# A hybrid decoder step on one core: squares of x spread out, latents copied early, the pool chain begun sooner

## The chip, the cores and the metric

One Trainium2 chip, one core of it. The metric is the device time of one execution in microseconds (us); the time before is the median of three runs. The engines are called TensorE (PE in the rows), VectorE (DVE), ScalarE (ACT), GpSimd (POOL) and SyncE (SP, which here only issues DMAs). PEld is TensorE's weight load.

## The reference

One layer of a decoder for 512 prompt tokens and 8 x 8 sample tokens (576 tokens in all), d_model 2048, everything in float32. What matters here is the front of it:

```
h = rms_norm(x) ; z = h @ w_in
q_a (512) | ckv (256) | krope (64) | u (512) | qm (512) | gate (2048) = split(z)
ckv = rms_norm(ckv) ; krope = rope(krope)          # the latents, outputs too
pool: per group g of 4, window w = 2, 4, 8, 16:
    diff = trailing_mean(u_g, w) - u_g ; y_g = (diff @ w_pool_g) * pool_scale
memory: k, v = split(rms_norm(mem) @ w_mem_kv)
out = x + concat(mla, pool, cross) * silu(gate) @ w_out ; final rms_norm
```

The row factor 1/rms of x is a number per token, so the kernel multiplies x (times the norm's weights) by w_in first and scales the products later. For that it needs the sum of squares of every row of x, at some time before the first scaling.

## The kernel before, in words

Every float32 product is made of three matmuls on two halves: a value is split into a high half (ScalarE copies it to the narrower matmul type) and a low half (VectorE subtracts the high half from it), and `product` (L91) adds high x high, high x low and low x high (L94 to L96). So each block of weights passes DMA, ScalarE, VectorE and TensorE in that order, through a few slots that come free when TensorE has used them.

The front stage (`front_stage`, L256) is one program per engine, written out by hand; each engine runs its own instructions strictly in order and waits on semaphores. TensorE's order is:

1. **Latents** (L957): ckv and krope for 576 tokens, six weight units, token blocks in five PSUM banks (`kv_bank`, L341). Banks 3, 4 and 5 hold three of these five.
2. Units 6 and 7, the two halves of the gate of pool group 0 (`half`, L1018).
3. **28 products** (`pair_product`, L976): 4 pairs of output blocks (q_a and u) times 7 terms, a multiplication of 2 x 2 blocks with 7 products instead of 8. The weight sums of a pair are made by VectorE (`first` to `fourth`, L714 to L744). The token side has four *turned* blocks t1 to t4: x times the norm's weights is written as four quarters q0 to q3 (`x_scaled`, 16 blocks of 128 x 576, L622 to L627, all on ScalarE), VectorE adds the quarters (`turned_sum`, L754: t1 = q1 - q0, t2 = q3 - t1, t3 = q3 - q1, t4 = q2 - t2), ScalarE makes the high halves (`turned_hi`, L570), VectorE the low ones (`turned_lo`, L768). The high halves lie on the quarters' memory, so one waits until the quarter is read. Product 2 of each pair uses t2, product 3 t1, product 4 t3 and product 6 t4. Products add into banks A, B and C, which alternate between banks 0 to 2 and 3 to 5, so pair 1 (products 7 to 13) needs the latents' banks; product 7 waits for their copies (`kv_raw`, L989). Within a pair a bank is copied out between two products: product 2 adds to bank B and waits until ScalarE's step 0 has copied what product 0 left there.
   After product 13 five small matmuls spread 1/rms over the partitions (*the broadcast*, L1048 to L1055); they wait for `x_diag` (L870), and that for the sums of squares.
4. Units idx 2 to 25 of `ORDER` (L57): halves f2 to f9 (gates of pool groups 1 to 3, cross queries) and memory units m0 to m15, with the transposes of the tails of u (L1061) and the four pool products (L1069 to L1080) between them.

ScalarE and VectorE walk through the 28 products as *steps*: at each step one bank copy or addition, then the halves of the weights of product step + 3 (`pair_hi` L575, `pair_lo` L746), then other work that is tied to a step number. ScalarE's extra work is `square_row` (L560): it waits until a 128 x 2048 row block of x has landed, squares it with a running sum, and issues the DMA of the next block, on its own queue, into the same buffer. VectorE copies the latents' banks out at step 6 (L855 to L861).

After the steps both walk through j = 5 to 27, which stands for the unit idx j. The dictionaries `DIFF_AT`, `PO_AT`, `BEND_AT` (L239 to L241) and `POOLED_AFTER` (L242) tie the pool chain to j or idx. For each group g: GpSimd adds window levels (L526 to L534), VectorE makes the difference and its halves (L914 to L930, six instructions), TensorE multiplies (after unit idx), VectorE scales the result (L908 to L913), GpSimd multiplies with gate and sigmoid (`close_gate`, L508). GpSimd begins group g + 1 when VectorE has ended the difference of group g.

Of the kernel before, what the change touches and what calls it, by code (L numbers as in the profile page):

```python
# [17 lines left out]
ALU = mybir.AluOpType  # L18
# [11 lines left out]
KD = D // P  # L30
# [206 lines left out]
SQUARE_AT = {1: 0, 4: 1, 5: 2, 6: 3, 8: 4}  # L237
Z_OUT_AT = {6: 1, 14: 2, 23: 3}
DIFF_AT = {6: 0, 13: 1, 17: 2, 20: 3}  # L239
PO_AT = {13: 0, 17: 1, 20: 2, 24: 3}  # L240
BEND_AT = {7: 0, 9: 1, 17: 2, 25: 3}  # L241
POOLED_AFTER = {9: 0, 13: 1, 16: 2, 20: 3}  # L242
# [13 lines left out]
def front_stage(nc, a, s, block):  # L256
# [3 lines left out]
    with ExitStack() as ctx:  # L260
# [119 lines left out]
        T_AT = {2: 0, 1: 1, 3: 2, 4: 3}  # L380
# [19 lines left out]
        def t_high(t):  # L400
            return thi[:, T_AT[t], :, :]

# [90 lines left out]
        def _(pool):  # L493
# [22 lines left out]
            for g in range(GR):  # L516
                if g == GR - 1:
                    close_gate(0)
# [28 lines left out]
            for g in range(1, GR):  # L547
                close_gate(g)
# [4 lines left out]
        def _(act):  # L553
# [69 lines left out]
            for k in range(KD):  # L623
                if k == 8:
                    ring_hi(KV_UNITS + 1)
                act.activation(fs[:, 2 * (k // 8):2 * (k // 8) + 2, k % 8, :], halves(xraw[:, k, :]), ACT.Identity,
                               scale=gx[:, k:k + 1]).then_inc(scaled, 1)  # L627
# [9 lines left out]
            for step in range(PRODUCTS):  # L637
# [13 lines left out]
                if step == 10:  # L651
                    act.wait_ge(chain, 1)
                    act.activation(rx[:, 2, :], rx[:, 1, :], ACT.Sqrt).then_inc(root, 1)
# [13 lines left out]
            for j in range(AHEAD + HI, FIRST + 2 - KV_UNITS):  # L667
# [7 lines left out]
                if j == 10:  # L675
# [23 lines left out]
        def _(dve):  # L699
# [54 lines left out]
            def turned_sum(t):  # L754

                if t != 1:
                    dve.wait_ge(t_sum, {2: 1, 3: 2, 4: 2}[t])
                dve.wait_ge(scaled, 8 if t == 1 else KD)
# [9 lines left out]
            def turned_lo(t):  # L768

                dve.wait_ge(st_hi, T_HI_COUNT[t])  # L770
                if t == 2:
                    dve.wait_ge(t_sum, 4)
# [35 lines left out]
            ring_lo(KV_UNITS)  # L808
            first(0)
            turned_sum(1)  # L810
            ring_lo(KV_UNITS + 1)
            second(0)
            third(0)
            turned_sum(2)
            turned_sum(3)
            pair_lo(0)
            fourth(0)
            pair_lo(1)
            turned_sum(4)
            turned_lo(2)  # L820
            pair_lo(2)
            turned_lo(1)

            for step in range(PRODUCTS):
# [30 lines left out]
                if step == 6:  # L855
                    dve.wait_ge(prep, 2)
                    dve.wait_ge(s.w_used, KV_UNITS)
                    dve.wait_ge(kv_low, 1)
                    dve.tensor_tensor(s.kvn[0:NS, 4, :], kv_bank(4)[0:NS], kv_tmp, ALU.add).then_inc(kv_raw, 1)
                    for r in range(4):  # L860
                        dve.tensor_copy(s.kvn[:, r, :], kv_bank(r)).then_inc(kv_raw, 1)  # L861
                if step == 9:
                    dve.wait_ge(sq, TT)
                    link(dve.tensor_scalar(rx[:, 1, :], rx[:, 0, :], 1.0 / D, EPS, ALU.mult, ALU.add))
                if step == 10:
# [30 lines left out]
            for j in range(AHEAD + HI, FIRST + 2 - KV_UNITS):  # L896
                if j == 8:
# [33 lines left out]
                if j == 7:  # L931
# [17 lines left out]
        def _(pe):  # L949
# [105 lines left out]
            for idx, (kind, k) in list(enumerate(ORDER))[AHEAD:]:  # L1055
# [5 lines left out]
                if idx == 6:  # L1061
# [2576 lines left out]
```

## Time and profile before

| | |
|---|---|
| median of three runs | 878.52 us (878.41 to 879.72) |
| the profiled execution's own time | 879.79 us |
| its span in the trace | 878.1 us |
| TensorE busy | 849.1 us, 97% |
| VectorE, ScalarE, GpSimd busy | 659.9, 502.3, 145.9 us |
| granted TensorE clock, mean | 0.988 of full speed |

The span is what the trace shows between the first and the last instruction; the execution's own time is 1.69 us more. Times in the rows are counted from the span's start. A matmul's row starts when it enters the engine, and rows of one engine overlap a little. In the timeline a bracket at the end of a row gives the idle time of the engine before that row and what ended it.

### The profile page before, as it was taken

How to read it: one execution, taken by the hardware profiler on the slowest of the kernel's cores; microseconds unless marked ns; L12 is line 12 of the kernel's file. 1: busy time of each engine (PE TensorE's matmuls, PEld its weight loads, DVE VectorE, ACT ScalarE, POOL GpSimd, SP SyncE). 2: the span in 40 equal slices, each digit the busy share in tenths (PEclk: the TensorE clock that was granted, in tenths of full speed). 3: DMA queues.
4: the chain of work that ended last, by engine and by line, in shares of the span. 5: the costliest groups of instructions: out<-in, count | busy, mean ns of one | idle time of the engine just before them, and what ended most of it. 6: DMA issues, size and time to landing. Idle time of an engine off the chain costs nothing.

```text
span 878.1 us, 15845 instructions
## 1 busy us (share of the span) xinstructions
PE 849.1 (97%) x5453; PEld 771.2 (88%) x5453; DVE 659.9 (75%) x1062; ACT 502.3 (57%) x819; POOL 145.9 (17%) x213
## 2 busy tenths in 40 slices
PE   9995899999899999999999999999999999999996
PEld 8995899988798999999999999888888788888885
DVE  6696487578945967989888976876778889474767
ACT  7774444464334456767766663667777556363446
POOL 0000000314610020323333332000000111111023
PEclk9998899999999999999999999999999999999999
DMA  8524422745357458888888864624117765988586
GB/s 336 193 77 144 140 96 91 264 142 188 120 198 295 159 189 260 276 259 263 248 256 265 261 215 142 236 85 156 37 48 294 197 198 122 234 245 253 124 158 216
DMA packets 64879, 168.57 MB, mean 192 GB/s; under 512 B 9672, under 2 KB 27657, under 8 KB 62808
## 3 DMA queue, kind: packets, MB, share of 16 engines
q1 hardware_dynamic: 52672, 126.46, 41.8%
q0 software_dynamic: 10752, 33.56, 16.7%
q10 hardware_dynamic: 1376, 7.54, 2.4%
q8 instruction: 44, 0.72, 0.3%
q14 instruction: 35, 0.29, 0.1%
HBM read 156.14 MB, written 11.50 MB: 191 GB/s over the span
## 4 chain that ended last, share of the span: by engine, by line
PE 88%; DVE 6%; ACT 3%; issue 2%; DMA 1%; ACTq 0%; DVEq 0%
PE front_acc L94 7%; PE z L94 7%; PE front_acc L96 7%; PE z L96 7%; PE z L95 7%; PE front_acc L95 7%; PE pa_s L94 4%; PE pa_s L96 4%; PE pa_s L95 4%; PE pa_qk L96 3%; PE pa_qk L95 3%; PE pa_qk L94 3%; PE pa_t L96 2%; PE pa_t L95 2%; PE pa_t L94 2%
## 5 line engine op out<-in xcount | busy, mean ns | idle before, releaser
L94 PE MATMUL z<-x_hi,w_hi 128*128 128x288 f32 x480 | 143.0, 298 | 0.0
L95 PE MATMUL z<-x_lo,w_hi 128*128 128x288 f32 x480 | 141.5, 295 | 0.0
L96 PE MATMUL z<-x_hi,w_lo 128*128 128x288 f32 x480 | 141.5, 295 | 0.0
L214 ACT ACTIVATE w_hi<-w_raw 128x1024 fp32r<-128x1024 f32 (+2 forms) x52 | 54.6, 1050 | 102.1 <-PE z L96 51.8
L1322 POOL DMA_DIRECT2D v_raw<-in_cache x128 | 69.1, 540 | 165.8 <-issue 164.2
L2352 ACT ACTIVATE o_hi<-o_raw 128x1024 fp32r<-128x1024 f32 x50 | 52.9, 1060 | 69.6 <-PE pa_s L3326 35.4
L94 PEld LDWEIGHTS z<-x_hi,w_hi 128*128 128x128 f32 x480 | 90.2, 188 | 2.7 <-issue 1.1
L95 PEld LDWEIGHTS z<-x_lo,w_hi 128*128 128x128 f32 x480 | 90.2, 188 | 1.7 <-issue 0.2
L221 DVE TENSOR_TENSOR w_lo<-w_raw,w_hi 128x1024 fp32r<-128x1024 f32 (+2 forms) x52 | 65.8, 1267 | 34.4 <-ACT w_hi L214 34.2
L96 PEld LDWEIGHTS z<-x_hi,w_lo 128*128 128x128 f32 x480 | 90.1, 188 | 0.0
L2606 DVE TENSOR_TENSOR o_lo<-o_raw,o_hi 128x1024 fp32r<-128x1024 f32 x50 | 60.9, 1220 | 34.4 <-ACT o_hi L2352 34.3
L94 PE MATMUL front_acc<-x_hi,w_hi 128*128 128x288 f32 x192 | 58.1, 303 | 15.4 <-DVE kvn L861 12.7
L96 PE MATMUL front_acc<-x_hi,w_lo 128*128 128x288 f32 x216 | 63.7, 295 | 0.0
L95 PE MATMUL front_acc<-x_lo,w_hi 128*128 128x288 f32 x192 | 57.7, 301 | 0.0
L2242 POOL DMA_DIRECT2D o_raw<-in_w_out x30 | 26.4, 915 | 165.6 <-DVE o_lo L2606 110.7
L94 PEld LDWEIGHTS front_acc<-x_hi,w_hi 128*128 128x128 f32 x192 | 37.1, 193 | 16.1 <-DVE kvn L861 13.0
L1506 DVE TENSOR_TENSOR k_lo<-k_raw,kt_hi 128x1024 fp32r<-128x1024 f32 x32 | 39.2, 1226 | 3.1 <-ACT kt_hi L1354 2.3
L96 PEld LDWEIGHTS front_acc<-x_hi,w_lo 128*128 128x128 f32 x216 | 40.7, 188 | 0.0
L1511 DVE TENSOR_TENSOR v_lo<-v_raw,v_hi 128x1024 fp32r<-128x1024 f32 x32 | 38.7, 1209 | 2.1 <-ACT v_hi L1360 2.1
L95 PEld LDWEIGHTS front_acc<-x_lo,w_hi 128*128 128x128 f32 x192 | 37.1, 193 | 0.1
L1360 ACT ACTIVATE v_hi<-v_raw 128x1024 fp32r<-128x1024 f32 x32 | 33.6, 1051 | 0.8 <-DMA v_raw<-in_cache 0.8
L1354 ACT ACTIVATE kt_hi<-k_raw 128x1024 fp32r<-128x1024 f32 x32 | 33.7, 1052 | 0.0
(628 smaller groups left out, 2539.9 us busy)
## 6 DMA issues: line engine op xcount, KB each, us to landing
k_raw<-in_cache SPq DMA_DIRECT2D x128, 192.0 KB, 3.3
w_raw<-in_w_feat SPq DMA_DIRECT2D x40, 512.0 KB, 4.4
v_raw<-in_cache POOLq DMA_DIRECT2D x128, 128.0 KB, 3.4
o_raw<-in_w_out POOLq DMA_DIRECT2D x30, 512.0 KB, 8.6
o_raw<-in_w_out SPq DMA_DIRECT2D x20, 512.0 KB, 8.5
w_raw<-in_w_mem_kv SPq DMA_DIRECT2D x16, 512.0 KB, 3.5
mix<-gate_spill SPq DMA_DIRECT2D x4, 1152.0 KB, 10.6
x_row<-in_x ACTq DMA_DIRECT2D x4, 1024.0 KB, 4.8
```

What stands on the lines that cost most here:

```text
L94: pe.matmul(out, a[0], b[0], start=start, stop=False, skip_group_check=onto)
L95: pe.matmul(out, a[0], b[1], start=False, stop=False, skip_group_check=onto)
L96: return pe.matmul(out, a[1], b[0], start=False, stop=stop, skip_group_check=onto)
L214: act.activation(hi_slot(s, u)[:, lo:w], s.wraw[:, raw_slot(u), lo:w], ACT.Copy).then_inc(s.w_hi, 1)
L221: dve.tensor_tensor(s.wlo[:, raw_slot(u), lo:w], s.wraw[:, raw_slot(u), lo:w], f32(hi_slot(s, u)[:, lo:w]), ALU.subtract).then_inc(s.w_lo, 1)
L1322: pool.dma_start(vraw[:, m % VRING, j, :], a["cache"][bass.ds(page, 1), :, 0:KVR].rearrange("o p c -> (o p) c")).then_inc(v_in[m % VRING], 16)
L1354: act.activation(kth[:, n % 2, :, :].rearrange("p c (j k) -> p j c k", j=4), keys_t(kraw, n), ACT.Copy).then_inc(kt_hi, 1)
L1360: act.activation(vh[:, m % HRING, :, :], vraw[:, m % VRING, :, :], ACT.Copy).then_inc(v_hi, 1)
L1506: dve.tensor_tensor(keys_t(klo, n), keys_t(kraw, n), f32(kth[:, n % 2, :, :]).rearrange("p c (j k) -> p j c k", j=4), ALU.subtract).then_i ...
L1511: dve.tensor_tensor(vlo[:, m % VRING, :, :], vraw[:, m % VRING, :, :], f32(vh[:, m % HRING, :, :]), ALU.subtract).then_inc(v_lo, 1)
L2352: act.activation(split_slot(u)[0][:], yt.raw_of(u), ACT.Copy).then_inc(y_hi, 1)
L2606: dve.tensor_tensor(lo_[:], yt.raw_of(u), f32(hi_[:]), ALU.subtract).then_inc(y_lo, 1)
```

## The change

- The squares of the row blocks of x move from steps 1, 4, 5, 6, 8 to steps 1, 3, 5, 7, 9. The factor's arithmetic on VectorE and the square root on ScalarE move one step later.
- The last six of the sixteen scaled blocks of x are made by VectorE, before its first weight sum, and no longer by ScalarE.
- The turned sums are made in the order t1, t2, t4, t3 instead of t1, t2, t3, t4, and are placed between other sums and halves differently; the high halves of t1 and t3 change places in memory.
- Four of the five copies of the latents' banks go from VectorE's step 6 to ScalarE's step 2; the fifth (an addition for the sample tokens) stays on VectorE and goes to step 2.
- The pool chain's places move to earlier units; the transposes of the tails come after unit idx 3 instead of 6, their copies on ScalarE at j = 7 instead of 10; `kv_n` (the latents' norm) goes from j = 8 to j = 10; the low half of w_pool from j = 7 to 6.
- GpSimd no longer closes the gate of group 0 before the windows of group 3, but after them.

```diff
-SQUARE_AT = {1: 0, 4: 1, 5: 2, 6: 3, 8: 4}
+SQUARE_AT = {1: 0, 3: 1, 5: 2, 7: 3, 9: 4}
+ACT_F = 10
-DIFF_AT = {6: 0, 13: 1, 17: 2, 20: 3}
-PO_AT = {13: 0, 17: 1, 20: 2, 24: 3}
-BEND_AT = {7: 0, 9: 1, 17: 2, 25: 3}
-POOLED_AFTER = {9: 0, 13: 1, 16: 2, 20: 3}
+DIFF_AT = {5: 0, 9: 1, 12: 2, 15: 3}
+PO_AT = {9: 0, 12: 1, 15: 2, 18: 3}
+BEND_AT = {7: 0, 10: 1, 17: 2, 25: 3}
+POOLED_AFTER = {5: 0, 8: 1, 11: 2, 15: 3}
...
-        T_AT = {2: 0, 1: 1, 3: 2, 4: 3}
+        T_AT, T_HI_AT = {2: 0, 1: 1, 3: 2, 4: 3}, {2: 0, 3: 1, 1: 2, 4: 3}
...
         (GpSimd)
             for g in range(GR):
-                if g == GR - 1:
-                    close_gate(0)
...
-            for g in range(1, GR):
+            for g in range(GR):
                 close_gate(g)
...
         (ScalarE)
-            for k in range(KD):
+            for k in range(ACT_F):
...
                 if step in SQUARE_AT:
                     square_row(SQUARE_AT[step])
-                if step == 10:
+                if step == 2:
+                    for r in range(4):
+                        act.activation(s.kvn[:, r, :], kv_bank(r), ACT.Copy).then_inc(kv_raw, 1)
+                if step == 11:
                     act.wait_ge(chain, 1)
                     act.activation(rx[:, 2, :], rx[:, 1, :], ACT.Sqrt).then_inc(root, 1)
...
-                if j == 10:
+                if j == 7:
                     act.wait_ge(tail, 1)
...
         (VectorE)
                 if t != 1:
-                    dve.wait_ge(t_sum, {2: 1, 3: 2, 4: 2}[t])
-                dve.wait_ge(scaled, 8 if t == 1 else KD)
+                    dve.wait_ge(t_sum, {2: 1, 4: 2, 3: 3}[t])
+                dve.wait_ge(scaled, 8 if t == 1 else ACT_F)
+                if t != 1:
+                    dve.wait_ge(x_lo, 2 * KD - ACT_F)
...
             ring_lo(KV_UNITS)
+            for k in range(ACT_F, KD):
+                dve.tensor_scalar(fs[:, 2:4, k % 8, :], halves(xraw[:, k, :]), gx[:, k:k + 1], None, ALU.mult).then_inc(x_lo, 1)
             first(0)
             turned_sum(1)
             ring_lo(KV_UNITS + 1)
+            turned_sum(2)
             second(0)
             third(0)
-            turned_sum(2)
-            turned_sum(3)
             pair_lo(0)
+            turned_sum(4)
             fourth(0)
             pair_lo(1)
-            turned_sum(4)
             turned_lo(2)
+            turned_sum(3)
             pair_lo(2)
             turned_lo(1)
...
-                if step == 6:
+                if step == 2:
                     dve.wait_ge(prep, 2)
-                    dve.wait_ge(s.w_used, KV_UNITS)
                     dve.wait_ge(kv_low, 1)
                     dve.tensor_tensor(s.kvn[0:NS, 4, :], kv_bank(4)[0:NS], kv_tmp, ALU.add).then_inc(kv_raw, 1)
-                    for r in range(4):
-                        dve.tensor_copy(s.kvn[:, r, :], kv_bank(r)).then_inc(kv_raw, 1)
-                if step == 9:
+                if step == 10:
                     dve.wait_ge(sq, TT)
                     link(...)
-                if step == 10:
+                if step == 11:
                     dve.wait_ge(root, 2)
                     rsqrt(...)
...
-                if j == 8:
+                if j == 10:
                     dve.wait_ge(tab, 16 * 5)
...
-                if j == 7:
+                if j == 6:
                     dve.wait_ge(wp_hi, 1)
...
         (TensorE)
-                if idx == 6:
+                if idx == 3:
                     pe.wait_ge(u_ready, 3 * GR)
```

## Rows read from the trace of the kernel before

**Rows 1.** The page, first part: busy time, share of the span and instructions of each engine.

```profile
PE 849.1 (97%) x5453; PEld 771.2 (88%) x5453; DVE 659.9 (75%) x1062; ACT 502.3 (57%) x819; POOL 145.9 (17%) x213
```

**Rows 2.** TensorE's waits: waiter <- releaser: us in total, times, longest us.

```profile
PE front_acc L94 <- DVE kvn L861: 12.7, 1, 12.7
PE front_acc L94 <- DVE w_lo L221: 3.5, 3, 2.6
```

**Rows 3.** TensorE's timeline: first matmul of products 2, 3, 7, 9, of the broadcast, of f6.

```profile
60.65 0.37 PE L94 MATMUL front_acc<-t_hi,w_hi 128*128 128x288 f32 x1 [1.84 <-ACT t_hi L573]
...
65.35 0.39 PE L94 MATMUL front_acc<-t_hi,w_hi_more 128*128 128x288 f32 x1
...
91.06 0.61 PE L94 MATMUL front_acc<-x_hi,w_hi 128*128 128x288 f32 x1 [12.72 <-DVE kvn L861]
...
99.83 0.30 PE L94 MATMUL front_acc<-t_hi,w_hi_more 128*128 128x288 f32 x1
...
115.73 1.23 PE L1052 MATMUL front_acc<-x_diag,ones 128*128 128x128 f32 x10
...
215.95 0.30 PE L94 MATMUL front_acc<-x_hi,w_hi 128*128 128x288 f32 x1
```

**Rows 4.** ScalarE's and VectorE's timelines while TensorE stood still, 84 to 91 us.

```profile
84.25 1.91 ACT L565 ACTIVATE x_row<-x_row 128x2048 f32<-128x2048 f32 x1 [4.46 <-DMA x_row<-in_x]
...
87.80 1.23 DVE L752 TENSOR_TENSOR slots_lo<-slots_raw,w_hi_more 128x1024 fp32r<-128x1024 f32 x1 [6.39 <-ACT w_hi_more L584]
...
89.34 1.66 DVE L861 COPY kvn<-front_acc 128x320 f32<-128x320 f32 x4
```

**Rows 5.** One microsecond of TensorE: stretch, length, busy (instructions), granted clock, DMA share, GB/s.

```profile
63.00:64.00 1.00, 1.00 (x6) 0.50 0.00 0
```

**Rows 6.** VectorE's and ScalarE's timelines before product 2, 37 to 61 us.

```profile
37.73 1.23 DVE L721 TENSOR_TENSOR w_raw<-slots_raw 128x1024 f32<-128x1024 f32 x1 [3.86 <-PE front_acc L970]
...
53.41 2.55 DVE L766 TENSOR_TENSOR t_raw<-x_scaled,t_raw 128x2304 f32<-128x2304 f32 x1
...
56.00 4.15 ACT L573 ACTIVATE t_hi<-t_raw 128x2304 fp32r<-128x2304 f32 x2 [1.71 <-DVE t_raw L766]
60.05 0.39 ACT L644 ACTIVATE zq<-front_acc 128x288 f32<-128x288 f32 x1
```

**Rows 7.** Groups by shape, 30 to 170 us: busy us, mean ns of one, idle before.

```profile
L626 ACT ACTIVATE x_scaled<-x_raw,g_x 128x576 f32<-128x576 f32 x16 | 10.9, 761 | 0.0
...
L875 DVE TENSOR_SCALAR kvn<-kvn,rx 128x320 f32<-128x320 f32 x4 | 1.3, 381 | 0.0
```

**Rows 8.** The five loads of row blocks of x, from issue to landing.

```profile
DMA to landing us min/median/max: 4.7/4.8/6.0
```

**Rows 9.** VectorE's and GpSimd's timelines in the pool chain, 167 to 237 us.

```profile
167.01 0.53 DVE L790 COPY u_last<-u_sample 128x64 f32<-128x64 f32 x1
...
210.15 1.55 DVE L779 SCALAR_TENSOR_TENSOR mem_lo<-mem_raw,g_mem,mem_hi 128x256 fp32r<-128x256 f32 x1
211.62 2.43 DVE L221 TENSOR_TENSOR w_lo<-w_raw,w_hi 128x1024 fp32r<-128x1024 f32 x2
...
216.40 0.68 DVE L920 SCALAR_TENSOR_TENSOR diff<-windows,u_first 128x512 f32<-128x512 f32 x1
...
218.84 0.48 DVE L779 SCALAR_TENSOR_TENSOR mem_lo<-mem_raw,g_mem,mem_hi 128x256 fp32r<-128x256 f32 x1
219.24 2.39 DVE L221 TENSOR_TENSOR w_lo<-w_raw,w_hi 128x1024 fp32r<-128x1024 f32 x1
...
230.29 1.20 DVE L920 SCALAR_TENSOR_TENSOR diff<-windows,u_last 128x512 f32<-128x512 f32 x1
...
235.75 1.22 DVE L221 TENSOR_TENSOR w_lo<-w_raw,w_hi 128x1024 fp32r<-128x1024 f32 x1
...
219.07 1.48 POOL L531 TENSOR_TENSOR windows<-u_last 128x711 f32<-128x711 f32 x1 [7.22 <-DVE diff_lo L930]
```

**Rows 10.** VectorE in one stretch: length, busy (instructions), granted clock, DMA share, GB/s.

```profile
180.00:220.00 40.00, 31.95 (x47) 1.00 0.51 158
```

More of the change, by code:

```diff
@@ L400, in t_high @@
         def t_high(t):
-            return thi[:, T_AT[t], :, :]
+            return thi[:, T_HI_AT[t], :, :]
         @block.sync
@@ L771, in turned_lo @@
                 if t == 2:
-                    dve.wait_ge(t_sum, 4)
+                    dve.wait_ge(t_sum, 3)
                 dve.tensor_tensor(t_low(t), t_raw(t), f32(t_high(t)), ALU.subtract).then_inc(st_lo, 1)
```

## The prediction, made before the changed kernel was run

> **What bounds the kernel now.** The page's first part says that TensorE is busy for 97% of the span [rows 1], so what can be won is what it loses to waits and to its clock. Next I read its waits: one of 12.7 us in the front stage, on VectorE's copies of the latents' banks, and three that sum to 3.5 us, on low halves of weights [rows 2]; the others are under 2 us each. The timeline places the long one: product 7 starts at 91.06 after 12.72 us of standstill [rows 3]. Five undisturbed products (9 to 13) take 115.73 - 99.83 = 15.90, so 3.18 each. Products 7 and 8 took 99.83 - 91.06 = 8.77 for 6.36: another 2.41 lost. Product 2 waited too, 1.84 us, and took 65.35 - 60.65 = 4.70 for 3.18, a loss of 1.52 [rows 3]. In that product the granted clock is 0.50 of 2.4 GHz, the lower level, after two idle microseconds [rows 5].
>
> What made the copies late shows a view of the two other engines: ScalarE waited 4.46 us for a row of x to land, squared it for 1.91, and only then made the high half of product 9; VectorE had idled 6.39 for that half and came to the copies at 89.34, 1.66 long [rows 4]. So the copies are 2 us of the wait, and the row's load and square, queued ahead of a weight half on ScalarE, are the rest.
>
> **The change, part by part.**
>
> *Copies and squares.* At step 2 ScalarE makes the four copies some 70 us into the span; on VectorE they took 1.66 [rows 4], and I take the same. Behind them on ScalarE stand step 3's bank copy and high half 6, wanted by products 5 and 6, three and six microseconds later; so this costs nothing, and if that cover were gone it would cost its 1.7. Product 7 then waits only for its own halves, of which the last follows VectorE's second weight sum, about half a microsecond before TensorE is there. Removed: 12.7 of standstill and the 2.4 of half clock behind it, **-15.1**.
>
> *Six scalings on VectorE.* The shape isn't in the trace on VectorE: a 128x320 scaling takes 0.38 there, the 128x576 one on ScalarE 0.76 [rows 7]. Six take 2.3 to 4.6; by width I take 0.55, so 3.3. They fall into the 3.86 that VectorE idles before its first weight sum at 37.73 [rows 6]: cost zero, at the upper bound 0.7. Without that idle time all of it would go on to product 2. ScalarE is freed of six, but waits for sums later anyway: no gain.
>
> *Order of the turned sums.* This is a loss that the diff doesn't announce. Product 2 adds to the bank that ScalarE's step 0 copies, and that copy stands on ScalarE behind the high halves of t3 and t4 (56.00, two of them 4.15 long, then the copy at 60.05) [rows 6]. Both wait for the fourth turned sum. Before, VectorE had done seven 1024-wide instructions and three 2304-wide ones from 37.73 until that sum began at 53.41. After, the fourth is t3 and ahead of it stand the same seven and four of 2304: t1, t2, t4 and the low half of t2. One more of 2.55 [rows 6]: the last sum ends 2.55 later, the copy and product 2 come 2.55 later, at 63.2: **+2.5**. That t2's own halves are ready earlier doesn't help, since the copy is now last. TensorE then stands 4.4 us and not 1.84. How long product 2 then runs at the low clock lies between its 4.70 and the 5.59 of product 7 (8.77 less one product) [rows 3]; the idle time is nearer to a longer one, so 5.5: **+0.8**.
>
> *Squares at every second step.* They are no longer in the way of the copies, but each still waits on ScalarE for its row, and four rows follow each other through one buffer. After the copy at 62.6 come two high halves and the first square, and the next row's load is issued at 66.8. The second comes behind step 3's copy and high half, at 73.5, and takes 2.1 with its accumulator read. Rows land 4.7 to 6.0 after issue [rows 8]; I take 4.8, and 5.4 for the one with two weight loads beside it. Squares then end at 75.6, 82.6, 90.1 and 97.0, while products 7, 9 and 11 start at 81.4, 87.8 and 94.1. Queued behind the squares are high halves 9, 11 and 13: half 9 is ready at 85, half 11 at 93, in time. The last square is not: behind it stands the bank copy that product 12 needs (0.3 late), then high half 13, and behind that on VectorE the rows' factor, which now follows step 11's weight sums: low half 13 until 99.7, addition and two sums until 102.8, low half 14 until 104.0, factor and five diagonals until 106.1. TensorE has ended product 13 at 104.0 and waits for the broadcast until 106.3: **+2.6** with the 0.3. Bounds: with all rows at 4.7, 0.8; with all at 6.0, about 5. From product 14 on everything has the spacing that it had.
>
> *Pool chain.* All moved instructions are the same in number, so only the collisions change. The eight transposes and two copies of the tails come three units earlier, behind f3: TensorE ends the broadcast at 116.8, fourteen products of 3.18 at 161.3 and the two halves f2 and f3, of two products' matmuls each, at 174.0, and VectorE has u ready at 167.5 [rows 9]. Zero; if u were late, the wait would be that lateness. kv_n moves two units back; on SP its stores stand ahead of the loads of units 20 and later, and are reached once idx 9 is used, while VectorE makes kv_n ahead of the low half for idx 10: in time by the order, closer than before. GpSimd's first gate comes behind the windows of group 3; ScalarE's third sigmoid (j = 17) waits for it, and behind that stand high halves, but GpSimd ends it some microseconds earlier than j = 17 by my count. The 3.5 of waiting [rows 2] is 2.6 before f7 and 0.9 before m2 and m8 together, of which I give m2 0.5: before m2 and f7 a difference stood ahead of the low half. Those two go: VectorE has no difference there any more. But group 3's difference now stands ahead of f6: after m8's low half (the first of the two from 211.62, so 212.8) come the scaling of group 2 (0.8), the difference (218.84 - 216.40 = 2.44 free of collisions) and the low half (1.22) [rows 9], until 217.3, and f6, which began at 215.95 [rows 3], some 0.2 later: 1.6. In place of 0.5 and 2.6 that is **-1.5**, with bounds -3.5 (no wait is left) and +1.5 (the difference takes 230.29 to 235.75, 5.46, as group 3's did).
>
> **Sum:** -15.1 + 2.5 + 0.8 + 2.6 - 1.5 = **-10.7 us**. The profiled execution took 879.79 (span 878.1), 1.27 above the median of 878.52; so 869.1 for such an execution, and a median of **867.8**. The later stages have TensorE as their bound and their own loads; I let them shift as a whole.
>
> *A rule against the pool part.* A window addition of GpSimd ran from 219.07 to 220.55; a low half that VectorE began at 219.24 took 2.39 for 1.22 and ended at 221.63, 1.08 after it, as if it had run only then; a memory half took 1.55 for 0.48 [rows 9]. The Trainium skill (page "SBUF — State Buffer", section "Who interferes with whom") says why: a VectorE instruction with two SBUF inputs and a GpSimd instruction that reads SBUF exclude each other for a whole instruction, and the later one is fully blocked. The rows agree; by that rule, were group 3's difference to meet the gates again, the sum would be -7.7.
>
> **The rivals.**
>
> A. *No new waits:* rows land early enough and the difference before f6 meets free time. For: it takes about half a microsecond less per row load. Against: 4.7 is the shortest landing seen. -10.7 - 2.6 - 1.6 = -14.9: **863.6**.
>
> B. *The collision goes along.* GpSimd closes gates 0 and 1 exactly when group 3's difference is made, which then takes 5.46 and not 2.44 [rows 9]: +3.0, **870.8**. Against: by my count gate 1 ends as the difference begins.
>
> C. *The squares' wait only moves*, so the change doesn't do what it says: spacing gives nothing, and low half 9 comes at 87.80 + 1.23 as before [rows 4], so TensorE, which could start it at 91.06 - 12.72 + 2 x 3.18 = 84.7, stands 4.5 there with the signal's delay. +4.5: **872.3**. Against: the third row load is issued at 75.6, nine microseconds before product 8 ends.
>
> D. *Slower: VectorE becomes the bound from m3 to f6.* The chain is squeezed from fourteen units into ten, with GpSimd beside it. If three differences (3.0 more each), seven low halves (1.17) and six memory halves (1.07) all collide [rows 9], that is 23.7 us; VectorE has 40 - 31.95 = 8.05 free there [rows 10]. 15.6 would come on top of -9.2 (the sum without the chain): +6.4, **884.9**. It decides once 17.3 of the 23.7 occur. Against: GpSimd's moved windows and gates fill only part of that stretch, and in the old trace only a few of the instructions there met them.
>
> **How the numbers follow.** Chances: forecast 0.55, A 0.16, B 0.14, C 0.07, D 0.05, and 0.03 that half of D eats the gain. A measurement can tell some 0.2% (1.8 us) from no change. Faster is the forecast with A, B and C, 0.92; same 0.03; slower 0.05. The range runs from 864.0, which leaves out half of A, to 872.5, which holds B and half of C: D, no change and those halves leave out 0.2. The forecast's bounds (rows, scalings, collisions) lie inside it.
>
> **What would show it.** Right: no standstill before product 7; one of some 4.5 before product 2, ended by ScalarE behind t_hi; one of about 2 before the broadcast, ended by VectorE's diagonals; waits before m8 and f6 but none before f7. Wrong: a standstill before product 9 or 11 ended by a high half behind a square (C); product 2 at 60.65 or earlier (my count of the order fails); several waits on low halves between m3 and f6 with VectorE instructions of 1.2 to 2.4 (B, D). I would be wrong most if ScalarE's step 2 came late because of product 2, since everything to product 14 hangs on it.

## The result and the profile after

The changed kernel takes 875.62 us (median of 20 executions, 872.63 to 879.20); the kernel before, in turns with it, 879.81 (20 executions, 878.41 to 882.85). The ratio is 0.9948, with a 95% interval of 0.9937 to 0.9958: faster by 0.5%, less than half of what was forecast. The profiled execution took 874.72 (span 873.0), 5.1 less than that of before.

TensorE's busy time, the first part of the page [rows 1], has hardly changed. What changed is its waits. First the page's line, then the view of TensorE's waits (waiter <- releaser: us in total, times, longest us), which answers to [rows 2]:

```profile
PE 849.8 (97%) x5453; PEld 771.7 (88%) x5453; DVE 661.7 (76%) x1064; ACT 499.5 (57%) x817; POOL 146.0 (17%) x213
```

```profile
PE front_acc L94 <- DVE w_lo L221: 5.4, 2, 4.1
PE front_acc L94 <- ACT t_hi L572: 4.4, 1, 4.4
PE front_acc L1055 <- DVE x_diag L873: 1.7, 1, 1.7
...
PE front_acc L94 <- ACT zq L643: 0.8, 1, 0.8
```

The wait of 12.7 for the latents' copies is gone. Against it stand 4.4 before product 2 (1.84 before), 0.8 before product 12 and 1.7 before the broadcast, and the waits on low halves have grown from 3.5 to 5.4. The timeline of TensorE answers to [rows 3]; it shows product 2, 3, 7, 9 and 12, the broadcast, products 14 and 15, m8, f6 and f8:

```profile
63.16 0.58 PE L94 MATMUL front_acc<-t_hi,w_hi 128*128 128x288 f32 x1 [4.38 <-ACT t_hi L572]
...
67.67 0.29 PE L94 MATMUL front_acc<-t_hi,w_hi_more 128*128 128x288 f32 x1
...
80.39 0.30 PE L94 MATMUL front_acc<-x_hi,w_hi 128*128 128x288 f32 x1
...
86.72 0.29 PE L94 MATMUL front_acc<-t_hi,w_hi_more 128*128 128x288 f32 x1
...
97.25 0.40 PE L94 MATMUL front_acc<-x_hi,w_hi_more 128*128 128x288 f32 x1 [0.85 <-ACT zq L643]
...
105.63 1.33 PE L1055 MATMUL front_acc<-x_diag,ones 128*128 128x128 f32 x10 [1.74 <-DVE x_diag L873]
...
106.77 0.47 PE L94 MATMUL front_acc<-x_hi,w_hi 128*128 128x288 f32 x1
...
111.57 0.30 PE L94 MATMUL front_acc<-x_hi,w_hi_more 128*128 128x288 f32 x1
...
205.65 0.47 PE L94 MATMUL front_acc<-w_hi,mem_hi 128*128 128x512 f32 x1 [1.31 <-DVE w_lo L221]
...
212.75 0.58 PE L94 MATMUL front_acc<-x_hi,w_hi 128*128 128x288 f32 x1 [4.06 <-DVE w_lo L221]
...
247.53 0.29 PE L94 MATMUL front_acc<-x_hi,w_hi 128*128 128x288 f32 x1
```

Set against the same points of before this says where the gain went. Product 14 started at 116.77 before (the broadcast's 115.73 and 1.04 more) and starts at 106.77 now: a lead of 10.0. Product 15 started at 120.01 and starts at 111.57: 8.4, since product 14 took 4.80 and not 3.24. The lead stays 8.4 to the end of f3. At f8 (252.77 before) it is 5.24, and so it stays to the end. So the pair stage delivered; 1.6 was lost in product 14, and 3.2 in the memory stretch: waits of 1.31 and 4.06 where before had 0.51, 0.35 and 2.64, and 7.98 for f6 (the pool product behind it starts at 220.73) where a half takes 6.39.

The long product 14 and the long f6 have the same reason. In TensorE's windows (stretch, length, busy with instructions, granted clock, DMA share, GB/s) the clock is at the lower level in product 2, as in [rows 5], and also in both of these, each time behind a wait:

```profile
63.00:64.00 1.00, 0.84 (x3) 0.50 0.00 0
...
108.00:109.00 1.00, 1.00 (x6) 0.50 0.00 0
...
214.00:215.00 1.00, 1.00 (x6) 0.50 0.00 0
```

What made low halves late in the memory stretch can be seen in the timelines of VectorE and GpSimd side by side, 200 to 212 us. Each line is start, us, engine, line, operation.

```profile
200.07 1.28 DVE L161 TENSOR_SCALAR rm<-rm 128x2 f32<-128x2 f32 x1
...
201.58 1.55 DVE L783 SCALAR_TENSOR_TENSOR mem_lo<-mem_raw,g_mem,mem_hi 128x256 fp32r<-128x256 f32 x1
203.06 2.44 DVE L221 TENSOR_TENSOR w_lo<-w_raw,w_hi 128x1024 fp32r<-128x1024 f32 x1
...
206.15 1.19 DVE L923 SCALAR_TENSOR_TENSOR diff<-windows,u_last 128x512 f32<-128x512 f32 x1
...
208.42 1.85 DVE L933 TENSOR_TENSOR diff_lo<-diff,diff_hi 128x576 fp32r<-128x576 f32 x1
210.19 2.41 DVE L221 TENSOR_TENSOR w_lo<-w_raw,w_hi 128x1024 fp32r<-128x1024 f32 x1
...
199.89 1.44 POOL L513 TENSOR_TENSOR pool_out<-pool_out,gate_first 128x576 f32<-128x576 f32 x1
201.40 1.45 POOL L515 TENSOR_TENSOR gate_first<-pool_out,gate_even 128x576 f32<-128x576 f32 x1
202.81 1.60 POOL L513 TENSOR_TENSOR pool_out<-pool_out,gates_front 128x576 f32<-128x576 f32 x1
204.49 2.29 POOL L515 TENSOR_TENSOR gates_front<-pool_out,gate_odd 128x576 f32<-128x576 f32 x1
208.21 1.44 POOL L513 TENSOR_TENSOR pool_out<-pool_out,gates_front 128x576 f32<-128x576 f32 x1 [1.43 <-ACT gate_even L689]
209.73 1.79 POOL L515 TENSOR_TENSOR gates_front<-pool_out,gate_even 128x576 f32<-128x576 f32 x1
```

GpSimd closes three gates from 199.89 on, six multiplications with one gap of 1.43. Beside them one step of the memory factor takes 1.28, the memory half 1.55, the low half for m8 2.44, group 3's difference 4.0 (206.15 to 210.2), and the low half for f6 2.41 and ends at 212.6, just before f6 starts. The first two were as slow before: the memory half took 1.55 [rows 9], and the step of the factor 1.29, beside the gate of group 0 (VectorE's and GpSimd's timelines of before):

```profile
208.62 1.29 DVE L161 TENSOR_SCALAR rm<-rm 128x2 f32<-128x2 f32 x1
...
208.46 1.43 POOL L512 TENSOR_TENSOR pool_out<-pool_out,gate_first 128x576 f32<-128x576 f32 x1
```

The low half for m8 was not: the two low halves there took 2.43 together [rows 9].

### The profile page after: what moved, and what is told of

It is laid out like the page before. It is cut to its first block, busy times and chain, and to the rows that moved or that the text cites. A ratio compares the mean times of both kernels' runs of the same rounds, so it can differ in the third digit from the quotient of the medians.

```text
span 873.0 us, 15846 instructions
## 1 busy us (share of the span) xinstructions
PE 849.8 (97%) x5453; PEld 771.7 (88%) x5453; DVE 661.7 (76%) x1064; ACT 499.5 (57%) x817; POOL 146.0 (17%) x213
## 4 chain that ended last, share of the span: by engine, by line
PE 89%; DVE 4%; ACT 3%; DMA 2%; issue 2%; ACTq 0%; DVEq 0%
PE front_acc L94 7%; PE front_acc L96 7%; PE front_acc L95 7%; PE z L94 7%; PE z L96 7%; PE z L95 7%; PE pa_s L94 4%; PE pa_s L96 4%; PE pa_s L95 4%; PE pa_qk L96 3%; PE pa_qk L95 3%; PE pa_qk L94 3%; PE pa_t L95 2%; PE pa_t L96 2%; PE pa_t L94 2%; PE ps_s L1730 2%
## 5 line engine op out<-in xcount | busy, mean ns | idle before, releaser
L221 DVE TENSOR_TENSOR w_lo<-w_raw,w_hi 128x1024 fp32r<-128x1024 f32 (+2 forms) x52 | 67.8, 1304 | 34.1 <-ACT w_hi L214 33.8
```

The lines of the kernel that those rows point to most:

```text
L221: dve.tensor_tensor(s.wlo[:, raw_slot(u), lo:w], s.wraw[:, raw_slot(u), lo:w], f32(hi_slot(s, u)[:, lo:w]), ALU.subtract).then_inc(s.w_lo, 1)
```

## The experiments

The expectations use letters for the theories. P: the pool chain's move gives gain back, because VectorE's work there meets GpSimd's gates. Q, its rival: the loss lies in the pairs, and the pool part costs nothing. R: the rows of x, loaded and squared one after the other, hold the end of pair 1. K: the lower clock behind short waits costs what the waits themselves don't. Each kernel was timed in turns with the kernel before, whose median lay between 879.45 and 880.80 us, so kernels are compared by their ratios to it, and a difference of 1 us between two medians says little.

**The parts of the change alone.** The changed kernel with the pool part undone (the four tables, the tails, kv_n, w_pool and the gate of group 0 as before; the diff shows the first):

```diff
-DIFF_AT = {5: 0, 9: 1, 12: 2, 15: 3}
+DIFF_AT = {6: 0, 13: 1, 17: 2, 20: 3}
...
```

> The changed kernel with its pool part undone (places of differences, scalings, sigmoids and pool products, tails, kv_n, low half of w_pool, GpSimd's first gate as before); only the part around the 28 products is left. Theory P (what is missing from the forecast was lost in the pool chain, where group 3's difference stands ahead of f6's low half): TensorE's waits before m2, m8 and f7 return to their 3.5 us of before, the waits of 1.3 and 4.1 us before m8 and f6 and the half clock in f6 are gone, and the kernel is some 8 to 9 us faster than before (ratio about 0.990), so 4 us faster than the whole change. Rival Q (the loss lies in the pairs, at the broadcast and in the clock behind it, and the pool part costs nothing): no better than the whole change, 4 to 5 us faster than before (0.995).

Measured: 876.23 us, ratio 0.9963 (0.9949 to 0.9976); the profiled execution 873.37. That isn't better than the change. TensorE's waits on low halves:

```profile
PE front_acc L94 <- DVE w_lo L221: 3.7, 2, 3.2
```

The longest, 3.16, is the old one before f7 [rows 2, 2.64 there], and here f7 takes 7.98 behind it, where it took 6.46 before. So the old order has a wait of its own there, with a clock loss behind it: P's number failed, and Q's came.

The kernel before with the pool part alone (the same places, as in the change):

```diff
-DIFF_AT = {6: 0, 13: 1, 17: 2, 20: 3}
+DIFF_AT = {5: 0, 9: 1, 12: 2, 15: 3}
...
```

> The kernel before with the pool part alone. Theory P: 3 to 5 us slower than before (ratio 1.003 to 1.006), product 7 still waits 12.7 us, and waits of about 1.3 and 4.1 us stand before m8 and f6. Rival Q: within 1 us of before, or up to 1.5 us faster as the forecast had it.

Measured: 882.57 us, ratio 1.0034 (1.0021 to 1.0046). The pool part alone makes the kernel slower. TensorE's waits on low halves:

```profile
PE front_acc L94 <- DVE w_lo L221: 5.6, 2, 4.1
```

They are 1.57 before m8 and 4.05 before f6, the same two as in the changed kernel, though they come 7.5 us later. Here P's number came and not Q's. The two experiments don't add up to one price of the pool part, because the old order also loses in the memory stretch once the pairs are faster.

The copies of the latents alone, in the kernel before (VectorE's step 6 loses them, and its addition goes to step 2):

```diff
                 if step in SQUARE_AT:
                     square_row(SQUARE_AT[step])
+                if step == 2:
+                    for r in range(4):
+                        act.activation(s.kvn[:, r, :], kv_bank(r), ACT.Copy).then_inc(kv_raw, 1)
...
```

> The kernel before with the latents' copies alone moved (four on ScalarE at step 2, the addition on VectorE at step 2); squares stay at steps 1, 4, 5, 6, 8. If the copies are what kept product 7 and the squares' waits only move behind them: no wait before product 7, but waits of 3 to 5 us each before products 9, 10 and 12 for halves queued behind squares; product 14 starts near 110 us and not 116.8; ratio 0.992 to 0.993. Rival (the copies were the whole of it): product 14 near 104 us, ratio 0.985.

Measured: 879.39 us, ratio 0.9983 (0.9967 to 0.9999). Product 7 has no wait, but product 9 stands 11.16. ScalarE's timeline says by what, and TensorE's that the wait ends with it:

```profile
92.58 1.91 ACT L565 ACTIVATE x_row<-x_row 128x2048 f32<-128x2048 f32 x1 [5.42 <-DMA x_row<-in_x]
...
95.19 0.41 ACT L644 ACTIVATE zq<-front_acc 128x288 f32<-128x288 f32 x1 [0.60 <-ACT x_row L565]
...
95.66 0.61 PE L94 MATMUL front_acc<-t_hi,w_hi_more 128*128 128x288 f32 x1 [11.16 <-ACT zq L644]
```

The bank copy of step 7 stands on ScalarE behind a square that waits for its row. Rival C of the prediction, a wait that only moves, is true of the copies alone.

The steps of the squares alone, in the kernel before (factor and square root one step later, as in the change):

```diff
-SQUARE_AT = {1: 0, 4: 1, 5: 2, 6: 3, 8: 4}
+SQUARE_AT = {1: 0, 3: 1, 5: 2, 7: 3, 9: 4}
...
```

> The kernel before with the squares alone moved to steps 1, 3, 5, 7, 9 (and the factor one step later); the copies stay on VectorE at step 6. If both parts are needed: product 7 still waits, some 6 to 8 us and not 12.7, for copies that VectorE reaches only behind low half 9; ratio 0.993 to 0.995. Rival (the row's square was the whole wait): product 7 waits under 2 us, ratio 0.985.

Measured: 876.30 us, ratio 0.9953 (0.9936 to 0.9970). Product 7 still waits (TensorE's waits):

```profile
PE front_acc L94 <- DVE kvn L861: 6.3, 1, 6.3
```

Half of the 12.7 goes with the squares' steps, the other half only when the copies go too; the copies alone gain 0.2%. That this one part gives as much as the whole change (its interval holds the change's 0.9948) shows that the rest of the change adds little in sum.

**The collision in the memory stretch.** First the place: the difference of group 3 goes one unit later, behind f6's low half.

```diff
-DIFF_AT = {5: 0, 9: 1, 12: 2, 15: 3}
-PO_AT = {9: 0, 12: 1, 15: 2, 18: 3}
-POOLED_AFTER = {5: 0, 8: 1, 11: 2, 15: 3}
+DIFF_AT = {5: 0, 9: 1, 12: 2, 16: 3}
+PO_AT = {9: 0, 12: 1, 15: 2, 19: 3}
+POOLED_AFTER = {5: 0, 8: 1, 11: 2, 16: 3}
```

> The changed kernel with one place changed: group 3's difference at j = 16 and no longer 15, so behind f6's low half (its pool product after idx 16, its scaling at j = 19). Theory P, in its narrow form (the difference's place ahead of f6 is what costs): the wait of 4.1 us before f6 falls under 1 us and the half clock there goes, the wait of 1.3 us before m8 stays; 4 to 6 us faster than the whole change, ratio to before about 0.989 to 0.990. Rival: VectorE is full over the whole stretch, so the wait only moves to m9 or m10; the ratio stays at 0.994 to 0.995.

Measured: 869.66 us, ratio 0.9893 (0.9878 to 0.9909). Before f6 there is no wait (it starts at 209.13), and 1.29 before m8 stays. Then the collision itself, with the difference where the change put it: GpSimd is held back until VectorE has made it.

```diff
             for g in range(GR):
                 pool.wait_ge(u_ready, 3 * (g + 1))
...
+            pool.wait_ge(diff, GR)
             for g in range(GR):
                 close_gate(g)
```

> The changed kernel with one wait more on GpSimd: it closes no gate until VectorE has ended group 3's difference (which stays ahead of f6's low half). It parts the collision from the mere place. If the collision with GpSimd's gates makes up most of the 4.1 us before f6 and the 1.3 before m8: the difference takes 2.5 and not 4.0, low half f6 1.2 and not 2.4, the memory factor 0.8 and not 2.7; m8's wait falls under 0.5, f6's to 1 to 1.5, without half clock; 4 to 5 us faster than the whole change (ratio to before 0.989 to 0.991). If the place alone does it: f6 still waits 3 us or more, ratio 0.993 to 0.995.

Measured: 869.16 us, ratio 0.9886 (0.9871 to 0.9901), from one added line. No wait on a low half is left in the stretch. Timelines of VectorE, GpSimd (its first gate) and TensorE (m8 and f6):

```profile
199.78 0.17 DVE L161 TENSOR_SCALAR rm<-rm 128x2 f32<-128x2 f32 x1
...
200.18 0.48 DVE L784 SCALAR_TENSOR_TENSOR mem_lo<-mem_raw,g_mem,mem_hi 128x256 fp32r<-128x256 f32 x1
200.58 1.22 DVE L221 TENSOR_TENSOR w_lo<-w_raw,w_hi 128x1024 fp32r<-128x1024 f32 x1
...
202.45 0.68 DVE L924 SCALAR_TENSOR_TENSOR diff<-windows,u_last 128x512 f32<-128x512 f32 x1
...
204.22 0.76 DVE L934 TENSOR_TENSOR diff_lo<-diff,diff_hi 128x576 fp32r<-128x576 f32 x1
204.89 1.22 DVE L221 TENSOR_TENSOR w_lo<-w_raw,w_hi 128x1024 fp32r<-128x1024 f32 x1
...
205.11 2.29 POOL L513 TENSOR_TENSOR pool_out<-pool_out,gate_first 128x576 f32<-128x576 f32 x1 [5.58 <-DVE diff_lo L934]
...
203.90 0.39 PE L94 MATMUL front_acc<-w_hi,mem_hi 128*128 128x512 f32 x1
...
206.71 0.29 PE L94 MATMUL front_acc<-x_hi,w_hi 128*128 128x288 f32 x1
```

The same instructions in the same order take 0.17 for 1.28, 0.48 for 1.55, 1.22 for 2.44, and the difference 2.44 (202.45 to 204.89) for 4.0. So it is not VectorE's amount of work that makes the waits, but GpSimd beside it; VectorE's order decides whether a unit of TensorE has to wait for it, as the run before this one shows. GpSimd's own work is later. ScalarE waits 3.0 for it, before the third gate's sigmoid, but no wait of TensorE comes of that. f8 starts at 239.90, 7.6 before the changed kernel; product 15 was only 0.3 earlier (111.30 for 111.57), so the rest was won in the memory stretch.

**The end of pair 1.** By the forecast two things stand in the way there: the order of turned sums before product 2, and the last square. ScalarE's step 0 first, with product 2's copy ahead of the high halves of t3 and t4:

```diff
-            turned_hi(3)
-            turned_hi(4)
             for step in range(PRODUCTS):
+                if step == 1:
+                    turned_hi(3)
+                    turned_hi(4)
```

> The changed kernel with ScalarE's step 0 (copy of bank B, high half 3) ahead of the high halves of t3 and t4. If product 2's wait is owed to that queue place: product 2 starts near 59.8 us and not 63.2 (a wait of about 1.1 and no half clock), and products 3 to 8 come 3 to 4 us earlier. Theory R (from there on the chain of row loads and squares sets the pairs' end, not TensorE): rows come only about 1.1 us earlier, so the broadcast does too, near 104.5 us, with a longer wait before it or before products 9 to 12; 1 to 2 us faster than the whole change, ratio to before 0.993. Rival (TensorE carries the gain through): 4 to 5 us faster than the whole change, ratio 0.990.

Measured: 873.37 us, ratio 0.9911 (0.9890 to 0.9932). That is faster than the change (0.9937 to 0.9958), by 2 us in the medians and 3 by the ratios; the interval holds both R's 0.993 and the rival's 0.990. In the profiled execution the product starts 3.4 earlier, and the wait comes back further on (timeline of TensorE, product 2, product 12, the broadcast):

```profile
59.80 0.37 PE L94 MATMUL front_acc<-t_hi,w_hi 128*128 128x288 f32 x1 [0.98 <-DVE w_lo L755]
...
97.34 0.40 PE L94 MATMUL front_acc<-x_hi,w_hi_more 128*128 128x288 f32 x1 [3.45 <-ACT zq L644]
...
105.72 1.33 PE L1056 MATMUL front_acc<-x_diag,ones 128*128 128x128 f32 x10 [1.75 <-DVE x_diag L874]
```

The broadcast is at 105.72, in the changed kernel at 105.63. That looks like R, but ScalarE's timelines show another reason. They give the issue of the last row's load (ACTq) and its square, in this kernel and then in the changed one:

```profile
87.17 0.53 ACTq L555 DMA_DIRECT2D x_row<-in_x  x1
...
94.84 1.91 ACT L564 ACTIVATE x_row<-x_row 64x2048 f32<-64x2048 f32 x1 [4.73 <-DMA x_row<-in_x]
```

```profile
89.52 0.53 ACTq L555 DMA_DIRECT2D x_row<-in_x  x1
...
94.75 1.92 ACT L564 ACTIVATE x_row<-x_row 64x2048 f32<-64x2048 f32 x1 [2.30 <-DMA x_row<-in_x]
```

The load is issued 2.35 earlier here, but its square begins 7.67 after the issue and not 5.23. So the rows do hold the end of the pair, as R says, but how much of the 3.4 gets through to it in other executions this one doesn't tell. The landing of a row also moves the end of the pair where nothing was changed: in four profiled executions whose front is the change's own (the change, pairs only, difference behind f6, gates held back) product 14 starts at 106.77, 107.28, 108.96 and 108.06. In this execution product 14 ran at full clock (3.24), which is worth 1.6 against the profiled execution of the change.

The factor and its diagonals at the start of VectorE's step 11, ahead of the addition that product 13 needs, and the square root at the start of ScalarE's. The block is the change's own, moved up:

```diff
+                if step == 11:
+                    dve.wait_ge(root, 2)
+                    rsqrt(dve, link, rx[:, 1, :], rx[:, 2, :], rx[:, 7, :], rx[:, 3, :])
...
                 if i in (1, 4, 5, 6):
                     dve.wait_ge(s.st_used, step + 1)
```

> The changed kernel with the rows' factor, its root and the five diagonals at the beginning of step 11, ahead of that step's weight sums and low half 14. If the broadcast's wait is owed to its place behind the sums: the 1.7 us before the broadcast goes, a wait of about 0.7 us before product 14 comes in its place, the half clock in product 14 (1.6 us) goes, and the kernel is 2 to 3 us faster than the whole change (ratio to before about 0.992). Rival: low half 14 comes 2 us later and gives all of it back, with a wait of 1.7 us or more before product 14; ratio 0.995.

Measured: 874.73 us, ratio 0.9947 (0.9934 to 0.9961). The broadcast has no wait of its own, but product 13 waits 1.63 for the addition, and the broadcast is at 106.12. The same block behind the addition and ahead of the two weight sums:

```diff
+                if step == 11:
+                    dve.wait_ge(root, 2)
...
                 if n_ + 1 < PAIRS:
                     if i == 3:
                         first(n_ + 1)
```

> The changed kernel with the rows' factor and the diagonals at step 11 between the addition (which product 13 needs) and the weight sums. In the run with the factor ahead of the addition the wait moved to product 13. If the order on VectorE is all that holds the broadcast: no wait before product 13, none before the broadcast, about 0.7 us before product 14 (low half 14 comes 2 us later), no half clock there; 1.5 to 2.5 us faster than the whole change, ratio 0.992 to 0.993. Rival (the chain of rows holds it anyway): product 14 no earlier than 106.5 us, ratio 0.995.

Measured: 875.72 us, ratio 0.9955 (0.9942 to 0.9969). The broadcast has no wait (105.69), but products 11, 12 and 14 wait 0.79, 1.73 and 0.77. Neither place gains in time over the change (0.9948). In the profiled execution of the second the fourth row's square began 7.48 after its load was issued (6.07 in that of the change), so what this place is worth with a row that lands in time stays open.

**The clock.** TensorE is kept at work during the waits before product 2, the broadcast, m8 and f6 by matmuls of ones into a bank (16 and 6 before the first two, 4 and 16 before m8 and f6):

```diff
+            def fill(n):
+                for _ in range(n):
+                    pe.matmul(ps[:, 7, 288:288 + P], s.ones[:], s.ones[:], start=True, stop=True, skip_group_check=True)
...
+                if m == 2:
+                    fill(16)
                 pair_product(m)
+                if m == 13:
+                    fill(6)
...
```

The fill before product 2 writes over 32 columns of the last prompt block's latents, so their krope isn't computed from x.

> The changed kernel with small matmuls of ones by ones, read by nobody, put on TensorE inside four of its waits: 16 before product 2, 6 before the broadcast, 4 before m8, 16 before f6 (0.21 us each, shorter in sum than each wait), so that the waits end when they did but TensorE is not idle in them. Theory K (part of what is missing is the half clock that follows these waits: 1.3 us in product 2, 1.6 in product 14, 1.6 in f6 in the profile of the whole change, more in slower executions): the granted clock stays at 1.00 from 10 us on, and the kernel is 3 to 5 us faster than the whole change (ratio to before 0.989 to 0.991), with less spread between executions. Rival (the clock is a small part): within 1.5 us of the whole change, 0.993 to 0.995.

Measured: 873.70 us, ratio 0.9917 (0.9896 to 0.9937). The waits end when they did (product 2 at 63.10, f6 at 212.44 against 212.75), but f6 then takes 6.46 and product 14 3.25. The six executions lie within 1.3 us of each other, at mean granted clocks of 0.995 to 0.998; the twenty of the changed kernel lie within 6.6, at 0.988 to 0.994. Some of the gain went into product 12, which took 4.81 for 3.3 behind a wait of 2.13 without a fill.

So in these four places the clock is worth some 2 us of the missing gain (875.62 to 873.70; 2.7 by the ratios), between the 3 to 5 that K expected and its rival's 1.5. That the waits are the rest follows only by subtraction.

**Together.** The copy of step 0 first, the factor between addition and weight sums, the difference of group 3 behind f6, and the memory factor at j = 21 instead of 14:

```diff
+                if step == 1:
+                    turned_hi(3)
+                    turned_hi(4)
...
-                if j == 14:
+                if j == 21:
                     dve.wait_ge(m_root, 1)
...
```

> The changed kernel with four moves together: ScalarE's step 0 ahead of the high halves of t3 and t4, the factor between addition and weight sums, group 3's difference behind f6's low half, the memory factor on VectorE at j = 21 and not 14. If the gains add: no wait over 1.5 us before product 9, one of 2 to 3.5 before product 12 (rows), none over 1 us from product 13 on, half clock in at most one place; 8 to 10 us faster than the whole change, ratio to before 0.984 to 0.986. If the chain of row loads takes back what the pairs win: like the run with the difference moved alone, 0.988 to 0.990.

Measured: 864.20 us, ratio 0.9829 (0.9816 to 0.9843): 15.3 us less than the kernel before in the same turns, and the five executions lie within 1.3 us, at clocks of 0.997 and 0.998. TensorE's waits in the front:

```profile
PE front_acc L94 <- DVE w_lo L755: 2.2, 4, 1.0
PE front_acc L94 <- ACT zq L647: 1.5, 1, 1.5
```

None is longer than 1.5. Product 14 starts at 104.63, f6 at 203.28 without a wait, f8 at 236.97. Product 14 is 2.1 earlier than in the changed kernel and 4.3 earlier than in the one with only the difference moved; the rows land differently in these executions, and no run parts the four edits. GpSimd held back was not tried in this version, nor a second buffer for the rows of x, which R would ask for next.

## Why the prediction was wrong, step by step

Faster was right; 867.8 and its range were not. The 7.8 us between forecast and median are 5.6 in the sum (-10.7 foretold, -5.1 in the traces), 1.3 because the 878.52 that the sum was laid on rose to 879.81 over 20 executions, and 0.9 by which the profiled execution lay under the median. The 5.6 are the pool chain's 4.7 (+3.2 for -1.5; the clock in f6 makes 1.6 of it) and product 14's 1.6, less 0.8 by which the pairs were better than foretold, and 0.1 that was lost behind f8. The signs given for being right all came: no standstill before product 7, 4.4 before product 2, 1.7 before the broadcast, waits before m8 and f6 and none before f7. So did the sign that was given for B, slow VectorE instructions beside waits on low halves. The places were right; the price of one of them was not.

- **Copies and squares, -15.1: right.** Product 7 starts without a wait at 80.39 (81.4 foretold), products 7 and 8 take 6.33. That both parts are needed, one experiment each shows. The copies on ScalarE took 1.41, not 1.66.
- **Six scalings: right.** They took 2.66 where 3.3 was taken, inside the idle time.
- **Order of the turned sums, +2.5: right to 0.05.** Product 2 is at 63.16 (63.2 foretold), behind ScalarE's high halves. Whether the whole of it is a loss at the end of the pair stays open: with the copy first the kernel is 2 to 3 us faster, but in the one profiled execution, with a late row, the broadcast isn't earlier. The sum counted it beside the rows' wait, though the rows' chain could have taken a part of it anyway.
- **The half clock in product 2, +0.8: too dear.** It took 4.51, even less than the 4.70 of before; with the gates held back, where nothing is different there and the wait is 4.38 as well, it took 5.69. This term belongs to the execution.
- **Squares at every second step, +2.6: right in this execution, and partly by luck.** 0.85 before product 12 and 1.74 before the broadcast make 2.6; the last square ended at 96.7 (97.0 foretold). Together the lead at product 14 is 10.0, where -9.2 was worked out; in the three other executions with this front it is 9.5, 7.8 and 8.7, as the rows landed. The 0.8 above belong to the execution too.
- **Pool chain, -1.5: the step that failed.** It stood on "the difference (218.84 - 216.40 = 2.44 free of collisions) and the low half (1.22)", and on "by my count gate 1 ends as the difference begins". The first took instructions that had met nothing before and kept their price at a place where GpSimd closes gates. The second was off by little (gate 1 ended at 206.78, the difference began at 206.15), but it left out what gate 1 does to the low half for m8 ahead of the difference, and gate 2, which met the difference's end and the low half for f6. Against the prices in the sum the low half for m8 took 1.2 more, the difference 1.6 more and the low half for f6 1.2 more: 4.0 of VectorE's time. The wait before f6 was 4.06 for 1.6, m8's 1.31 for 0.4: +1.9 in waits where -1.5 stood. This is rival B in kind, given 0.14, but larger: B priced the difference alone, at +3.0 where 1.6 came, and had neither the two low halves nor the clock behind the wait. With the gates held back both waits are gone, which shows the cause. The rule of the Trainium skill (page "SBUF — State Buffer", section "Who interferes with whom") that the prediction weighed, a VectorE instruction with two SBUF inputs and a GpSimd one that reads SBUF excluding each other, fits: the difference took 2.44 alone, 4.0 beside the gates. The 1.28 for 0.17 stands at a TENSOR_SCALAR with one tensor input, which the rule in these words doesn't cover, and no run here looks further.
- **A term that was missing: the clock behind the new waits.** The sum let product 2 alone run at the lower level. Product 14 behind the wait of 1.74 and f6 behind 4.06 lost 1.6 each, in the profiled execution. With the idle time filled both ran at full clock (3.25 and 6.46). For product 14 it is also chance: of five executions with this wait it lost 1.6 in two.
- **The rivals.** A, 863.6, would need both new waits gone, and no run did just that; the combined version, with other edits besides, comes to 864.2. C is true of the copies alone. D fell: the kernel is faster, and only the waits before m8 and f6 stand in the stretch.

## What to carry to other kernels

Price an instruction by the neighbour it will have at its new place, not by the one it had: count what GpSimd runs there from its own releaser on, and if its work is off the path, a wait that holds it back until VectorE's urgent instructions are done costs one line (5.5 us gained here by the ratios, 6.5 in the medians). On an engine that keeps its order, each instruction that waits for a DMA is a gate for all that stands behind it, so removing the last wait in a chain of loads only shows the next. A new wait of TensorE of 1.7 to 4.4 us needs a second term for the clock behind it, 0 to 2.8 us here, and a wait that was removed may be covered by a later one that nobody touched. Where a DMA's landing decides, one profiled execution is not enough: the same front ended its pair up to 2.2 us apart (product 14 at 106.77 and 108.96), as much as the copy first gained.

## What the runs showed of the hardware that was not expected

The lower clock behind a wait is not settled by the wait's length. Behind 1.74 or 1.75 before the broadcast product 14 took 4.80 and 4.78 in two profiled executions (the change; pairs only) and 3.24 in three others (difference behind f6; copy first; gates held back). At f7, 2.64 and 3.09 were followed by 6.46 and 6.45 for the half, 3.16 and 3.17 by 7.98 and 7.96; at f6 waits of 4.1 by about 7.98 in four kernels and by 9.2 in one (factor first). Product 12 took 4.81 behind a wait of 2.13 (fills) and 3.29 behind one of 3.45 (copy first). Of the twenty executions of the change the longest, 879.20, has a mean granted clock of 0.988 and the shortest, 872.63, one of 0.993: 0.005 of 873 us is 4.4 of the 6.6 between them. In between the order is looser.

The delay that GpSimd gives a VectorE instruction does not grow with it: 1.1 for one of 0.17 us (1.28), 1.1 for one of 0.48 (1.55), 1.2 for one of 1.22 (2.44). Each began about 0.2 after one of GpSimd's multiplications had begun (200.07 after 199.89, 201.58 after 201.40, 203.06 after 202.81) and lost a little less than what was left of that (1.26, 1.27 and 1.35). So a short instruction can lose as much as a long one. Not every instruction there is hit: group 2's scaling, which reads PSUM, took its 0.81 at 205.42 in the midst of a multiplication (204.49 to 206.78).
